# A hybrid decoder step on one core: the recurrent branch's mixing begun earlier, and a new order of the work between value pages

## The reference

```python
p = x @ w_in       # -> q_sb, k_sb, v_sb, q_mem, p_rw, g_sb, g_mem, g_rw
# stick-breaking attention over 16 cached pages of 128 tokens for each sample row, and over the prompt itself
o = einsum('bhqk,bkhd->bqhd', w[..., :past], v_past) + einsum('bhqk,bkhd->bqhd', w[..., past:], v_new)
# memory attention, 4 heads x 128, 256 memory rows
o_mem = softmax(q_mem . mem_k * MEM_SCALE) . mem_v
# recurrent branch (RWKV-7)
prev = concatenate([shift0, p_rw[:, :-1]]);  xs = p_rw + mu_rw * (prev - p_rw)
r, k, v, w_lo, a_lo, g_lo = split(xs)
decay = exp(-exp(-softplus(-(w_decay0 + tanh(w_lo) @ w_decay2)) - 0.5))
a = sigmoid(w_aaa0 + a_lo @ w_aaa2);  g = sigmoid(g_lo) @ w_gate2
kk = k * rw_k_k;  kk = kk / max(sqrt(sum(kk * kk)), 1e-12);  k_mod = k * (1 + (a - 1) * rw_k_a)
# ... scan over the tokens, group norm, bonus = sum(r * k_mod * rw_r_k) * v
merged = sigmoid(g_sb) * (o_sb @ w_sb_o) + sigmoid(g_mem) * (o_mem @ w_mem_o) + sigmoid(g_rw) * (o_rw @ w_rw_o)
h = LN1(ALPHA * x + merged @ w_out);  y = LN2(ALPHA * h + MoE(h))      # top 4 of 32 experts
```

## Time and profile before

| | |
|---|---|
| median of 3 runs | 1527.87 us (1526.35 to 1528.28) |
| profiled execution | 1529.42 us, span 1527.5 us |
| mean granted clock of TensorE | 0.989 |
| busy: TensorE / weight load / VectorE / ScalarE / GpSimd | 1465.0 / 747.0 / 572.5 / 265.7 / 141.9 us |
| read from memory | 528.92 MB, 349 GB/s over the span |

### The profile page before, as it was taken

The page is one execution under the profiler, slowest core; times in us unless marked ns, Lnnn a source line. Parts: engine busy times, 40 slices in busy tenths (PEclk is TensorE's granted clock), DMA queues, the critical chain, the costliest instruction groups (busy, mean ns, idle before and its releaser), DMA issues.

```text
span 1527.5 us, 22221 instructions
## 1 busy us (share of the span) xinstructions
PE 1465.0 (96%) x8374; PEld 747.0 (49%) x8374; DVE 572.5 (37%) x994; ACT 265.7 (17%) x534; POOL 141.9 (9%) x267
## 2 busy tenths in 40 slices
PE   7998999899999999999999999999999999999995
PEld 6887645457777755434434434434434434434431
DVE  1999957824445643211211211211211211211214
ACT  1111523222212111111111111111111111111102
POOL 5332232230210101000000000000000000000000
PEclk9999999999899999999999999999999999999998
DMA  9899997994111457999999999999999999999994
GB/s 346 311 367 335 349 363 281 350 308 149 29 57 57 148 246 265 423 428 428 428 429 428 429 429 429 429 427 429 429 428 429 428 429 429 428 428 428 428 426 184
DMA packets 67898, 534.30 MB, mean 350 GB/s; under 512 B 8588, under 2 KB 9687, under 8 KB 35063
## 3 DMA queue, kind: packets, MB, share of 16 engines
q1 hardware_dynamic: 48774, 471.52, 74.7%
q0 software_dynamic: 8656, 41.97, 7.8%
q10 hardware_dynamic: 10400, 19.92, 3.6%
HBM read 528.92 MB, written 4.46 MB: 349 GB/s over the span
## 4 chain that ended last, share of the span: by engine, by line
PE 76%; DVE 8%; issue 7%; DMA 6%; ACT 2%; POOL 0%; POOLq 0%; DVEq 0%; SPq 0%; ACTq 0%
PE bank L814 73%; DVE ring L2002 5%; PE bank L815 3%; DMA early<-in_w_gate_up 2%; DMA arena<-in_w_gate_up 2%; DMA arena<-in_state_rw_wkv 1%; DVE early L2008 1%; DVE arena L2366 0%; ACT memT L1938 0%; DMA arena<-in_x_sample 0%; DVE arena L2342 0%; DVE arena L2460 0%; ACT arena L1666 0%; DVE arena L2070 0%; DVE arena L2351 0%
## 5 line engine op out<-in xcount | busy, mean ns | idle before, releaser
L814 PE MATMUL bank<-arena 64*64 64x64 f32 (+9 forms) x2738 | 290.7, 312 | 7.3 <-DVE arena L2077 2.2
L2568 DVE TENSOR_SCALAR arena<-bank 128x256 f32<-128x256 f32 x64 | 26.9, 421 | 629.9 <-PE bank L814 629.9
L814 PE MATMUL bank<-projT,ring 128*128 128x264 f32 x1056 | 255.0, 396 | 4.7 <-DMA ring<-in_w_in 1.9
L814 PEld LDWEIGHTS bank<-arena 64*64 64x64 f32 (+5 forms) x2738 | 183.5, 155 | 127.0 <-issue 114.8
L814 PE MATMUL bank<-ring,projT 128*64 128x512 f32 x1024 | 229.7, 595 | 0.9 <-DMA ring<-in_w_gate_up 0.9
L814 PEld LDWEIGHTS bank<-projT,ring 128*128 128x128 f32 x1056 | 198.8, 193 | 45.9 <-issue 4.1
L814 PE MATMUL bank<-ring,memT 128*64 128x512 f32 (+2 forms) x640 | 168.8, 603 | 5.8 <-ACT memT L1938 4.5
L814 PEld LDWEIGHTS bank<-ring,projT 128*64 128x64 f32 x1024 | 70.6, 137 | 149.9 <-issue 148.1
L814 PE MATMUL bank<-projT 128*64 128x512 f32 (+2 forms) x544 | 118.8, 581 | 0.4 <-DMA projT<-in_w_gate_up 0.4
L1934 ACT ACTIVATE arena<-arena 128x256 f32<-128x256 f32 x64 | 26.7, 417 | 410.8 <-DVE arena L2568 410.8
L814 PEld LDWEIGHTS bank<-ring,memT 128*64 128x64 f32 (+2 forms) x640 | 51.6, 143 | 81.5 <-issue 70.1
(11 more groups left out here) (291 smaller groups left out, 1073.5 us busy)
## 6 DMA issues: line engine op xcount, KB each, us to landing
ring<-in_w_gate_up SPq DMA_DIRECT2D x64, 2048.0 KB, 20.2
projT<-in_w_gate_up SPq DMA_DIRECT2D x32, 2048.0 KB, 21.1
ring<-in_w_down SPq DMA_DIRECT2D x32, 2048.0 KB, 24.6
arena<-in_w_gate_up SPq DMA_DIRECT2D x16, 2048.0 KB, 20.5
projT<-in_w_down SPq DMA_DIRECT2D x16, 2048.0 KB, 23.2
early<-in_w_gate_up SPq DMA_DIRECT2D x16, 2048.0 KB, 22.1
ring<-in_cache_sb_k SPq DMA_DIRECT2D x64, 256.0 KB, 6.1
ring<-in_cache_sb_k POOLq DMA_DIRECT2D x64, 256.0 KB, 5.7
```

The source lines that it names most:

```text
L814: mm = lambda out, l, r, first, last, **k: pe.matmul(out, l, r, start=first, stop=last, **k)
L2568: ts(g_, chunk[:, 0:512:2], LIMIT, None, ALU.min).then_inc(sem("g_ready"), 1)
```

## The change

Nothing is computed in another way. Three things move:
- `mix` writes its scratch into `memT` instead of `T1` and is defined earlier. VectorE calls `mix(12)` behind the second causal weight and `mix(4)` and `mix(0)` behind the last; the norm input of kk (`kk_sq`) comes before the first `cached_scores`, and the `cached_scores` and `memory_max` are spread anew. A second count of `mixed` tells GpSimd that `mix(8)` is done.
- TensorE's order, and the bank plan with it: pages 10 and 11 before the first causal values; `dec`, `aaa` and `kn` ahead; queries and scores between pages; the last scores turned behind `branches(64, 72)`. Both calls of `keep_warm` (2 matmuls ahead of `dec`, 6 ahead of `bon`: `early=6`) are left out.
- ScalarE's order follows; `memory_weights(3)` stands behind the `so_s` move, and the exponentials of the decays behind the move of `("o", 0, 3)`.

```diff
-    after_gate = {5: ("dec", "aaa", "gr"), 6: ("kn",), 7: ("bon",)}
+    after_gate = {4: ("dec", 0, "aaa", "kn"), 5: ("gr", 1), 7: ("bon", 2, 3)}
...
@@ gpsimd
-            g.wait_ge(sem("kk_sq"), 1)
+            g.wait_ge(sem("mixed"), 2)
@@ tensor: low_rank
-                    if t == 0 and nm == "dec":
-                        keep_warm(b, 2)
@@ tensor
+            sample_values(10, 11)
             values(0)
-            sample_values(10, 11)
             values(1)
             sample_sum(1)
...
             values(3)
             memory_scores(0)
             memory_query(0)
+            branches(36, 40)
             sample_values(14, 15)
-            branches(36, 40)
             sample_sum(2)
 
+            sample_values(16, 17)
+            memory_turn(0)
+            low_rank("dec")
             memory_query(1)
-            memory_turn(0)
+            sample_values(18, 19)
+            memory_values(0)
+            low_rank("aaa")
+            memory_query(2)
+            pe.wait_ge(sem("masks"), 7)
+            over_heads("kn", T1, "kk_sq")
+            sample_sum(3)
             branches(40, 44)
-            sample_values(16, 17)
-            memory_values(0)
+            sample_values(20, 21)
+            memory_query(3)
+            memory_scores(1)
             branches(44, 48)
-            memory_scores(1)
-            memory_query(2)
-            sample_values(18, 19)
-            low_rank("dec")
-            memory_query(3)
-            sample_sum(3)
-
-            low_rank("aaa")
+            low_rank("gr")
+            sample_values(22, 23)
+            sample_sum(4)
+            sample_values(24, 25)
             memory_turn(1)
-            sample_values(20, 21)
-            low_rank("gr")
             branches(48, 52)
             memory_values(1)
+            sample_values(26, 27)
             branches(52, 56)
             memory_scores(2)
-            sample_values(22, 23)
-            sample_sum(4)
-
-            pe.wait_ge(sem("masks"), 7)
-            over_heads("kn", T1, "kk_sq")
-            memory_turn(2)
             memory_query(4)
             branches(56, 60)
-            sample_values(24, 25)
+            sample_values(28, 29)
+            sample_sum(5)
+            branches(60, 64)
+            memory_turn(2)
+            over_heads("bon", T1, "rk_prod")
+            memory_query(5)
+            sample_values(30, 31)
             memory_values(2)
-            memory_query(5)
-            branches(60, 64)
             memory_scores(3)
-            sample_values(26, 27)
-            sample_sum(5)
-
-            over_heads("bon", T1, "rk_prod", early=6)
-            memory_turn(3)
+            sample_sum(6)
             memory_query(6)
-            sample_values(28, 29)
-            memory_values(3)
-            memory_query(7)
-            sample_values(30, 31)
-            sample_sum(6)
             sample_sum(7)
...
+            memory_turn(3)
             row_to_features("so_sT", "so_s")
+            memory_query(7)
+            memory_values(3)
...
             branches(64, 72)
+            pe.wait_ge(sem("zm"), 1)
+            b = start("mzT")
...
+            branches(72, 76)
             pe.wait_ge(sem("mps"), 1)
             b = start("mpTs")
...
-            branches(72, 80)
+            branches(76, 80)
@@ scalar
+            gate_sums(0, (4,))
             act.wait_ge(sem("arena_clear"), 1)
             memory_weights(0)
...
             act.wait_ge(sem("mixed"), 1)
...
+            memory_turned(0)
             for t in range(4):
                 move(("dec", t), LD[:, t, :], lambda b: b[:, 0:T], ACT.Sigmoid, bias=col(DE0 + t))
+            memory_values(0)
             for t in range(4):
                 move(("aaa", t), AA[:, t, :], lambda b: b[:, 0:T], ACT.Sigmoid, bias=col(AA0 + t))
             for t in range(4):
+                move(("kn", t), T2[:, t, :], lambda b: b[:, 0:T], ACT.Sqrt)
+            gate_sums(0, (5,))
...
             memory_turned(2)
             memory_values(2)
-            gate_sums(0, (7,))
+            move("so_s", orow[0:NB, :], lambda b: b[0:NB, :])
             memory_weights(3)
             memory_turned(3)
@@ vector
             def mix(g0):
...
-                d = T1[:, 0:n, :]
+                d = memT[:, 0:n, :]
...
             causal_weights(0)
             causal_weights(1)
+            gone(v, "shift_in")
+            gone(v, ("mv", 0))
+            gone(v, ("mv", 1))
+            mix(12)
+            v.sem_inc(sem("mixed"), 1)
             keep_own(2)
             causal_weights(2)
             causal_weights(3)
...
+            mix(4)
+            mix(0)
             memory_max(0)
...
             link(per_tile(KK, Kx, KKp))
             tt_(T1, KK, KK, ALU.mult).then_inc(sem("kk_sq"), 1)
-            memory_max(2)
-            memory_norm(2)
-            keep_own(5)
+            memory_norm(0)
+            cached_scores(0)
+            keep_own(3)
+            mix(8)
+            v.sem_inc(sem("mixed"), 1)
+            cached_scores(1)
+            cached_scores(2)
+            keep_own(4)
 
             for t in range(4):
                 gone(v, ("kn", t))
             link(ts(T2, T2, 1e-12, None, ALU.max))
             v.reciprocal(T2[:, 0, :], T2[:, 0, :])
-            cached_scores(4)
             v.reciprocal(T2[:, 1, :], T2[:, 1, :])
+            memory_max(1)
             v.reciprocal(T2[:, 2, :], T2[:, 2, :])
-            cached_scores(5)
             link(v.reciprocal(T2[:, 3, :], T2[:, 3, :]))
             link(tt_(KK, KK, T2, ALU.mult))
+            cached_scores(3)
+            memory_norm(1)
...
             per_tile(T1, T1, RKp).then_inc(sem("rk_prod"), 1)
-            memory_max(3)
-            memory_norm(3)
+            keep_own(5)
+            memory_max(2)
+            cached_scores(4)
+            memory_norm(2)
             keep_own(6)
...
             link(tt_(AA, KK, AA, ALU.mult))
+            cached_scores(5)
+            memory_max(3)
+            keep_own(7)
+            memory_norm(3)
+            cached_scores(6)
             for t in range(4):
                 gone(v, ("dec", t))
...
-            cached_scores(6)
             cached_scores(7)
-            keep_own(7)
```

More of the change, by code:

```diff
@@ L142, in psum_plan @@
         add(("pv", b), 6 + b % 2)
-    after_gate = {5: ("dec", "aaa", "gr"), 6: ("kn",), 7: ("bon",)}
+    after_gate = {4: ("dec", 0, "aaa", "kn"), 5: ("gr", 1), 7: ("bon", 2, 3)}
     for i, name in enumerate(beside()):
         add(name, 3 if i < KT else (3, 7)[i % 2])
-        if i in after_gate:
-            add(("mo", i - 5), 4)
-            for nm in after_gate[i]:
+        for nm in after_gate.get(i, ()):
+            if nm in range(MH):
+                add(("mo", nm), 4)
+            else:
                 for t in range(4):
                     add((nm, t), (3, 4)[t % 2])
-    add(("mo", 3), 4)
     for h in range(MH):
@@ L1127, in _ @@
-            memory_turn(3)
+            sample_sum(6)
             memory_query(6)
-            sample_values(28, 29)
-            memory_values(3)
-            memory_query(7)
-            sample_values(30, 31)
-            sample_sum(6)
-            sample_sum(7)
-            pe.wait_ge(sem("zm"), 1)
-            b = start("mzT")
-            for mt in range(2):
-                last = tr(b[0:32, mt * P:mt * P + P], zm[:, mt, :])
-            done("mzT", last)
+            sample_sum(7)
             def row_to_features(name, row):
@@ L1154, in _ @@
             branches(64, 72)
+            pe.wait_ge(sem("zm"), 1)
+            b = start("mzT")
+            for mt in range(2):
+                last = tr(b[0:32, mt * P:mt * P + P], zm[:, mt, :])
+            done("mzT", last)
+            branches(72, 76)
             pe.wait_ge(sem("mps"), 1)
@@ L1790, in _ @@
             for t in range(4):
+                move(("kn", t), T2[:, t, :], lambda b: b[:, 0:T], ACT.Sqrt)
+            gate_sums(0, (5,))
+            for t in range(4):
                 move(("gr", t), GG[:, t, :], lambda b: b[:, 0:T])
+            memory_weights(1)
             memory_turned(1)
@@ L1796, in _ @@
             memory_weights(2)
-            for t in range(4):
-                move(("kn", t), T2[:, t, :], lambda b: b[:, 0:T], ACT.Sqrt)
+            gate_sums(0, (7,))
             memory_turned(2)
             memory_values(2)
-            gate_sums(0, (7,))
+            move("so_s", orow[0:NB, :], lambda b: b[0:NB, :])
             memory_weights(3)
             memory_turned(3)
+            move("so_sT", pT[:, Q0:Q0 + 4, NP_TOK:T], lambda b: b[:, 0:32].rearrange("p (t b) -> p t b", t=4))
             memory_values(3)
+            for dt in range(2):
+                move(("o", 0, dt), mergedT[:, dt, :], lambda b: b[:, 0:T])
+            act.wait_ge(sem("mem_max_s"), 1)
+            b = take(act, "mzT")
+            act.activation(mps[0:32, :], b[0:32, 0:256], ACT.Exp, scale=MEM_SCALE, bias=mst[0:32, 8:9],
+                           accum_out=mst[0:32, 9:10]).then_inc(freed_by("mzT"), 1)
```

(13 more changed lines are left out.)

40 lines of the change are left out of this document (removed).

## The result

The changed kernel takes 1536.53 us, median of 20 runs (1531.39 to 1543.91); the kernel before, in the same comparisons, 1528.37 (20 runs). The ratio is 1.0044, 95% interval 1.0029 to 1.0060: slower by 6.7 us (the two medians lie 8.2 apart), where 0.3 us less was forecast and the range ended at 1532.5. The profiled execution took 1537.13 us, span 1535.3, mean granted clock 0.984.

What follows compares the result with a forecast made beforehand. TensorE's own order was taken to bound the kernel. Of 15 us gained before pages 26 and 27 the late keys left 1; with the end stretch the sum was −0.3 us, 1527.6, range 1521.5 to 1532.5.

Steps and rivals of the forecast that it cites:

- Bottleneck and carrying over: TensorE bounds the kernel; whatever it gains or loses before the state tiles are turned carries to the end one for one.
- Part 1: Early mixing in memT: 1.9 to 2.2 us gained, then lost waiting for pages 12 and 13; page 13 left at 229.2.
- Part 2: New order up to page 25: kk norm sums at about 250.2, cached_scores(3) ending 267.4 to 267.9, 5 us later than before.
- Part 3: Pages 26 and 27 come behind the late keys: TensorE idles 7 us, and of the 15 us only 1 is left.
- Part 4: Stretch behind page 27: ScalarE's order binds, zm signal at 315.6, memory values start at 320.7, before 320.96.
- The rule on the clock: Transfer waits close the clock gate, so the 7 us wait and two later ones each bring slow stretches; sum left unchanged.
- the prediction's 15 us of work and idle time to be saved: TensorE's idle times and warm-up instructions between 200 and 321 us, together 15 us that are no needed work.
- Rival D: The clock: two slow stretches on TensorE's path cost +2.6 us, time 1529.9; chance 0.08.
- C: Rival: keys clog the queue for pages behind them, page 27 lands at 286.0 instead of 281.3, +4.7, 1532.3; chance 0.2.

## Why the prediction was wrong

The chain was the predicted one, keys late behind cached_scores(3) and page 26 late behind the keys. Its sizes were not: the way to the keys' issue and the landing of page 26 each took 4.3 us more than the sum had. Side by side, in us from the start of the span:

| | predicted | measured | late by |
|---|---|---|---|
| page 13 done | 229.2 | 231.35 | 2.2 |
| norm sums of kk start | 250.2 | 255.15 | 5.0 |
| second keys issued | 268.2 | 272.52 | 4.3 |
| page 26 read | 279 | 287.62 | 8.6 |
| sample_sum(7) done | 304.0 | 312.7 | 8.7 |
| memory values start | 320.7 | 328.42 | 7.7 |

**Bottleneck and carrying over.** Right: a delay of 7.5 at the memory values is 7.4 at the states and 7.8 in the span.

**Part 1, the first step that failed.** Right in sense: values(0) needed no idle time (218.84), and the early 2 us were given back before pages 12 and 13. But page 13 was read 16.5 behind page 8 instead of 15.5, 1.0 late, and the clock fell behind the two waits: page 13, values(3) and memory_scores(0) took 1.87, 1.48 and 1.87 (229.48 to 234.70) where full speed is 0.93, 0.81 and 0.97: 2.5 more. The sum had nothing for a clock here. In part this was bad luck with the execution: the prediction's prices put page 14 at 21.0 behind page 8, it took 24.5, and of the six kernels with the same program up to there four took 23.1 to 25.5 and two 20.6 and 21.2, as priced. What makes the difference stays open. That pages 14 and 15, asked for 2 us earlier, share the full engines with page 13 is a possible cause that no run tests.

**Part 2.** The list to the kk norm sums was right in its prices; its waits were 1.08 + 1.43, where 1.7 stood. With that and part 1 the norm sums start at 255.15, and cached_scores(3) ends at 272.5 instead of 267.4 to 267.9. From the norm sums to its end it took 17.3, as predicted (17.2 to 17.7).

**Part 3, the second step that failed.** Page 26 was put 10.8 behind the keys' first issue (268.2 to 279); it took 15.1. The price of a landing, 5.0 to 5.5, came from the earlier trace rows, with the argument that the queues were not full there and that SyncE's had been empty here. The empty queue did not help, and the first reason does not hold: in the kernel before, the window in which those pages were issued shows full engines too:

```profile
228.00:234.00 6.00, 5.76 (x45) 3.02 (x46) 2.60 (x7) 1.40 (x5) 2.14 (x4) 1.00 1.00 386
```

What differed is how much was asked for at once. Here four page places had come free within 4 us, so pages 26 to 29 and the keys were under way together, 6.3 million bytes, and 5.6 million were moved before page 26 was read. The right sum was bytes by bandwidth, and the earlier trace rows had the rate (380 GB/s at a DMA share of 0.97). Leaving out the keys' bytes showed it (6.0 us less from issue to read); moving the keys, or freeing them early, moved the wait or took little off. With spaced pages the interval was 12.5 with late keys and 15.9 with early ones, so there too a page took far longer than 5; what spacing gives is that the engines work while they were idle before (DMA share 0.33 from 256 to 264, with spaced pages 0.96 and, with late keys, 0.89). The Trainium skill (DMA: Bandwidth & Descriptors, Queues, rings and completion order) says that each DMA engine turns round between the queues that have work, packet by packet; so GpSimd's halves of pages 28 and 29 take their share ahead of SyncE's halves of 26. The trace agrees in so far as GpSimd's halves, issued at 276.1 to 279.5, took 5.6 to 6.0 to land and SyncE's, issued at 275.5 to 279.2, 9.1 to 10.8; it does not show the packets' order.

Both pages ran at half clock, not one, but the sum had given them 4.0 us, for page 27 to land, and they took 3.57. Only the K-steps behind them, 2.70 instead of 1.87, were not in it.

**Part 4.** Right in place and nearly in size. TensorE waited 2.42 for memory_norm(3), which stood behind the so_s move; from sample_sum(7)'s end (312.7) to cached_scores(7)'s end (322.46 + 1.22 on VectorE, 323.7) it took 11.0, where 11.6 was put. The experiment with the softmax moved ahead took the wait away.

**The rule on the clock.** The Trainium skill (TensorE: Matmul & The Clock Gate, HAM oscillation) was right for the long wait: filled, it gave 2.1 us behind page 26. For the two short waits before pages 12 and 13 the rows go both ways: page 13 was slow behind waits of 2.83 and 1.44 and not behind 2.02 and 1.42. Against the removal of the warm-ups the rule did not count: without them the kernel before is not slower (0.9986), since they filled waits for VectorE and ScalarE that stay. For the same reason the prediction's 15 us of work and idle time to be saved were not all there to save in the old order; they also leave out a wait of 2.00 that the old trace has at 292.37. What made the changed kernel cold were new waits. Rival D, with 2.6 us and a chance of 0.08, was too small and should have been a term of the sum. (Its time should read 1530.2, which is 1527.6 + 2.6, not 1529.9.)

**The rivals and the range.** C was near the size of its term: it had page 27 landing 17.8 behind the keys' first issue where the forecast had 13.1, and the last piece of page 27 landed 16.3 behind it (279.2 + 9.6). But it had half the mechanism: not the keys clog the queue, the burst does, keys and four pages. C and D together give 7.3 above the forecast. They were taken as alternatives, but a longer wait and a slow stretch go together, and the range had room for one of them only. That 7.3 comes close to what was measured is in part chance, since the 4.3 us on the way to the keys are in neither.

## What to carry to other kernels

Where pages stream through a few places that are refilled as they are read, space the reads by what the transfers need. Four reads in a row do not fetch anything sooner: they leave the DMA engines idle ahead and ask for 4 MB at once behind. Price a transfer by all bytes that are under way at that time over the full rate, not by the landing time of a transfer that had fewer beside it; and ask of each forecast wait of TensorE what the slow stretch behind it costs. Before a difference of stretches is put down to an edit, look whether it arises where the edit has any effect: here 4.9 us between the two kernels with spaced pages arose where their programs were the same. Behind that point early keys were worth 1.3 us, the spaced order 7.6, and both 9.4.

## What the runs showed of the hardware

The clock fell behind waits as short as 2.83 and 1.44 us in a row (granted 0.75 and 0.82 in the windows around), and the work behind ran at half speed, 1.2 GHz, for some 5 us (229.48 to 234.70). At the same place of the same program page 13 was slow (1.80 to 1.94) in five executions, in which the wait before page 12 was 2.29 to 4.23, and at full speed (1.06) in two, behind 1.41 and 1.43 and behind 2.02 and 1.42. With the first wait filled by 6 matmul instructions page 13 ran at full speed in three executions, and in a fourth it still took 1.84 instead of 1.07. From memory 410 to 420 GB/s were moved with the 16 engines full, through two queues at once. In such a stretch the halves of pages that GpSimd issued landed in 5.6 to 6.0 us and those of SyncE, which stood behind the keys in its queue, in 9.1 to 10.8.
